# Two transformer blocks on one core: the second block's attention scores from rounded parts of queries and keys

## What is computed

```python
proj = u @ w_in[l]
qa, ka, va, qb, kb, vb, g = jnp.split(proj, SPLITS, axis=-1)
qa = rope(qa.reshape(B, Lp, SWA_Q_HEADS, HEAD_DIM), pos)
ka = rope(ka.reshape(B, Lp, SWA_KV_HEADS, HEAD_DIM), pos)
...
qb = rope(qb.reshape(B, Lp, DIFF_HEADS, 2, HEAD_DIM), pos)
kb = rope(kb.reshape(B, Lp, DIFF_HEADS, 2, HEAD_DIM), pos)
...
o_swa = windowed_gqa_sink_attention(qa, ka, va, attn_sink[l], pos, is_real)
...
o_diff = differential_attention(qb, kb, vb, lam, lambda_init, diff_subln_gain[l], is_key)
gates = jax.nn.sigmoid(g + b_gate[l])
g_swa, g_diff = gates[..., :D_MODEL], gates[..., D_MODEL:]
merged = g_swa * (o_swa @ w_branch_swa[l]) + g_diff * (o_diff @ w_branch_diff[l])
h = h + rms_norm(merged @ w_out[l], post_mix_gain[l])
```

## Time and profile before

| | |
|---|---|
| median of 3 runs | 877.63 us (877.02 to 877.80) |
| profiled execution, its own time | 877.45 us |
| its span, first to last instruction | 875.6 us |
| TensorE busy | 868.0 us, 99% |
| VectorE, ScalarE, GpSimd busy | 623.7 (71%), 459.2 (52%), 46.2 us (5%) |
| granted TensorE clock | 0.998 |
| DMA | 156.75 MB, 179 GB/s on average |

### The profile page before, as it was taken

One profiled execution on the slowest core, in us unless ns is written; L12 is line 12 of the kernel. 1 busy time (PEld: TensorE's weight loads), 2 busy tenths in 40 slices (PEclk: granted clock), 3 DMA queues, 4 the chain that ended last, 5 costly groups with the idle time before them and its releaser, 6 DMA issues.

```text
span 875.6 us, 13035 instructions
## 1 busy us (share of the span) xinstructions
PE 868.0 (99%) x4820; PEld 731.3 (84%) x4820; DVE 623.7 (71%) x987; ACT 459.2 (52%) x735; POOL 46.2 (5%) x83
## 2 busy tenths in 40 slices
PE   9999999999999999999999999999999999999997
PEld 6887788888888888889998777777888888888886
DVE  6867777765876666668855888787766876666665
ACT  6546534334644444454556777677643654444443
POOL 1000010000200000002000000132300100000000
PEclk9999999999999999999999999999999999999999
DMA  9955344553565555353683335323274365555541
GB/s 328 412 207 187 129 160 144 192 192 144 190 242 190 189 195 188 142 190 104 207 300 106 123 123 170 145 100 142 97 265 175 119 228 189 183 192 192 186 143 48
DMA packets 26830, 156.75 MB, mean 179 GB/s; under 512 B 3600, under 2 KB 5136, under 8 KB 9376
## 3 DMA queue, kind: packets, MB, share of 16 engines
q1 hardware_dynamic: 24048, 148.71, 47.6%
q10 hardware_dynamic: 2736, 7.42, 2.4%
HBM read 151.45 MB, written 1.05 MB: 174 GB/s over the span
## 4 chain that ended last, share of the span: by engine, by line
PE 99%; DMA 0%; DVE 0%; DVEq 0%; SPq 0%; ACTq 0%; ACT 0%; issue 0%
PE ps L495 19%; PE ps L497 18%; PE ps L496 18%; PE ps L661 8%; PE ps L646 8%; PE ps L665 4%; PE ps L642 4%; PE ps L674 4%; PE ps L1639 2%; PE ps L676 2%; PE ps L530 1%; PE ps L1574 1%; PE ps L1598 1%; PE ps L1593 1%; PE ps L1588 1%; PE ps L1283 1%
## 5 line engine op out<-in xcount | busy, mean ns | idle before, releaser
L1742 DVE TENSOR_TENSOR wlo<-raw,whi 128x2048 fp32r<-128x2048 f32 x134 | 306.7, 2290 | 151.7 <-ACT whi L783 151.4
L783 ACT ACTIVATE whi<-raw 128x2048 fp32r<-128x2048 f32 x134 | 256.4, 1914 | 182.8 <-PE ps L497 110.8
L495 PE MATMUL ps<-whi,xT 128*128 128x512 f32 x192 | 76.8, 400 | 0.0
L497 PE MATMUL ps<-whi,xT 128*128 128x512 f32 x192 | 75.0, 391 | 0.0
L496 PE MATMUL ps<-wlo,xT 128*128 128x512 f32 x192 | 74.8, 390 | 0.0
L495 PE MATMUL ps<-whi,fT_h 128*128 128x512 f32 x128 | 50.2, 392 | 0.0
L496 PE MATMUL ps<-wlo,fT_h 128*128 128x512 f32 x128 | 49.8, 389 | 0.0
L497 PE MATMUL ps<-whi,fT_l 128*128 128x512 f32 x128 | 49.8, 389 | 0.0
L495 PE MATMUL ps<-x_all,whi 128*128 128x272 f32 x160 | 46.6, 291 | 0.0
L496 PE MATMUL ps<-x_all,whi 128*128 128x272 f32 x160 | 46.2, 289 | 0.0
L497 PE MATMUL ps<-x_all,wlo 128*128 128x272 f32 x160 | 46.2, 289 | 0.0
(11 more groups left out here) (347 smaller groups left out, 1834.5 us busy)
## 6 DMA issues: line engine op xcount, KB each, us to landing
raw<-weights SPq DMA_DIRECT2D x134, 1024.0 KB, 4.8
kswap<-kraw SPq DMA_DIRECT2D x52, 68.0 KB, 2.0
cst<-consts SPq DMA_DIRECT2D x1, 1371.0 KB, 13.0
raw<-weights SPq DMA_DIRECT2D x4, 256.0 KB, 5.5
raw<-weights SPq DMA_DIRECT2D x2, 512.0 KB, 7.2
gate_a<-gain_rows ACTq DMA_DIRECT2D x2, 512.0 KB, 7.7
gate_r<-gain_rows ACTq DMA_DIRECT2D x2, 512.0 KB, 6.7
gate_s<-gain_rows ACTq DMA_DIRECT2D x2, 512.0 KB, 6.6
```

Source lines behind the costliest of these rows:

```text
L495: pe.matmul(o, lh, rh, start=first, stop=False)
L497: return pe.matmul(o, ll, rh, start=False, stop=last)
L783: act.activation(whi[s][:], raw[s][:], ACT.Copy).then_inc(split_hi, 1)
L1742: dve.tensor_tensor(wlo[s][:], raw[s][:], whi[s][:], ALU.subtract).then_inc(split_lo, 1)
```

## The change

**Parts instead of halves.** Queries and keys are no longer left as fp32 on 64 rows. VectorE's turning ends in `kraw` (L2343 of the changed kernel for keys, L2334 for queries, `rot_ok`). ScalarE rounds that to a high part (`keys_high`, `queries_high`, L1102, L1111, `rot_hi`), GpSimd subtracts to get the low part (L1354 for keys, L1359 for queries), and it is GpSimd that now signals `kt_ok`. The operands of the scores have 128 rows: the query tile holds the high part over the low part (or low over high for the other head of a pair), the key tile the same part twice. DMAs bring them there. Two rounded matmuls with the same weights, one with the keys' high part and one with their low part, give all four products.

**The way through memory.** A turned key of both parts is stored to a tensor in HBM (`key_parts`, `store_keys`, one DMA of 0.56 MB, five in all), and loaded from there into two key tiles of a ring (`load_shared_keys`, 2 x 6 DMAs, and `load_keys`, 8 x 4 DMAs, the latter when the scores that used the tile are done). Queries go from SBUF to SBUF (`store_queries`, 8 x 4 DMAs). All 81 are on SP's queue, between the loads and the swaps. From the third key on, `keys_high` waits until the store of the key two before it has landed, since its tile is used again.

**Order.** Query blobs are now 6, 7, 9, 10, 12, 13, 15 and 17 (the fifth of the queries in the third place), value blobs 5, 8, 11, 14 and 16. Gates and up projections alternate: 18 to 21 gates, 22 to 25 the first up projection, 26 to 29 gates, 30 to 33 the second. The units go by pairs of queries tiles (`unit_place`). The rows of the gates' bias are fetched later (steps 38 and 54), behind a wait for the scores, whose tiles they overwrite.

```diff
-QUERIES = (6, 7, 12, 13, 14, 15, 16, 17)
+QUERIES = (6, 7, 9, 10, 12, 13, 15, 17)
+QUERY_PLACE = (0, 1, 4, 2, 3, 5, 6, 7)
+VALUES = (5, 8, 11, 14, 16)
...
-VALUES_AT = {12: 0, 18: 1, 20: 2, 22: 3, 24: 4}
+VALUES_AT = {12: 0, 18: 1, 24: 2, 30: 3, 34: 4}
...
+            def store_keys(i):
+
+                sp.wait_ge(kt_ok, i + 1)
+                sp.dma_start(kd[i], knat[i % 2][:].bitcast(F32)).then_inc(kd_out[i % 2], 16)
...
+            def load_keys(cc):
+
+                sp.wait_ge(u_sc, 2 * cc + 14 if cc else 8)
+                for u in range(2):
+                    for copy in range(2):
+                        sp.dma_start(kB[cc % 2][copy * DH:(copy + 1) * DH, 2 * u:2 * u + 2, 0:KEYS],
+                                     kd[1 + cc // 2, u * DH:(u + 1) * DH, :, cc % 2, :]).then_inc(kb_in[cc % 2], 16)
...
+            def keys_high(i):
+
+                act.wait_ge(rot_ok, i + 1)
+                if i >= 2:
+
+                    act.wait_ge(kd_out[i % 2], 16 * (i // 2))
+                act.activation(knat[i % 2][:, 0], kraw[i % 2][:], ACT.Copy).then_inc(rot_hi, 1)
...
+                if q in (4, 6, 8, 10, 12):
+                    keys_high(q // 2 - 2)
...
+            for i in range(5):
+                pool.wait_ge(rot_hi, i + 1)
+                pool.tensor_tensor(knat[i % 2][:, 1], kraw[i % 2][:], knat[i % 2][:, 0],
+                                   ALU.subtract).then_inc(kt_ok, 1)
...
-                    pe.wait_ge(kt_ok, query_made(U))
+                    if t == 0:
+                        pe.wait_ge(q_in[query_of(U)], 64)
+                        pe.wait_ge(kb_in[key_slot(U)], keys_loaded(U))
...
-                    qT = qsT if U < S_UNITS else qbT
+                    qT, kT = qs if U < S_UNITS else qd, kB[key_slot(U)]
                     for u in range(2):
-                        half = slice(u * DH, (u + 1) * DH)
-                        kT = ksT[half, cc // 4, :] if U < S_UNITS else kbT[half, cc, :]
-                        m = pe.matmul(ps[:, 4 + u, 0:KEYS], qT[half, cc, t * P:(t + 1) * P], kT, start=True, stop=True)
+                        for v in range(2):
+                            m = pe.matmul(ps[:, 4 + u, 0:KEYS], qT[u][:, cc, t * P:(t + 1) * P].bitcast(F32R),
+                                          kT[:, 2 * u + v, 0:KEYS].bitcast(F32R), start=v == 0, stop=v == 1)
```

More of the change, by code:

```diff
@@ L123, in values_blob @@
 def values_blob(i):
-    return 7 + i if i else 5
+    return VALUES[i]
 def swaps_before(m2):
@@ L409, in build @@
         v_ps = sem("v_ps")
+        rot_ok = sem("rot_ok")
+        rot_hi = sem("rot_hi")
         kt_ok = sem("kt_ok")
+        kd_out = [sem("kd_out0"), sem("kd_out1")]
+        kb_in = [sem("kb_in0"), sem("kb_in1")]
+        q_in = [sem(f"q_in{j}") for j in range(len(QUERIES))]
         ql_ok = sem("ql_ok")
@@ new lines, in load_keys, with store_queries @@
+            def load_keys(cc):
+                sp.wait_ge(u_sc, 2 * cc + 14 if cc else 8)
+                for u in range(2):
+                    for copy in range(2):
+                        sp.dma_start(kB[cc % 2][copy * DH:(copy + 1) * DH, 2 * u:2 * u + 2, 0:KEYS],
+                                     kd[1 + cc // 2, u * DH:(u + 1) * DH, :, cc % 2, :]).then_inc(kb_in[cc % 2], 16)
+            def store_queries(m2):
+                i = QUERIES.index(m2)
+                sp.wait_ge(kt_ok, 5 + i + 1)
+                j = QUERY_PLACE[i]
+                both = slice(2 * (j % 4), 2 * (j % 4) + 2)
+                hi, lo, dst = qh[i % 2], ql[i % 2], qs if j < 4 else qd
+                low, high = slice(0, DH), slice(DH, P)
+                sp.dma_start(dst[0][low, both, :], hi[low].bitcast(F32)).then_inc(q_in[j], 16)
+                sp.dma_start(dst[0][high, both, :], lo[low].bitcast(F32)).then_inc(q_in[j], 16)
+                sp.dma_start(dst[1][low, both, :], lo[high].bitcast(F32)).then_inc(q_in[j], 16)
+                sp.dma_start(dst[1][high, both, :], hi[high].bitcast(F32)).then_inc(q_in[j], 16)
@@ L2481, in weight_stream @@
     out += blob_tokens(w, at[2], 256)
-    for q in range(2):
-        out += blob_tokens(qa, 256 * q, 256)
-    for q in range(4):
-        out += blob_tokens(w, at[5] + 256 * q, 256)
-    for q in range(2, 4):
-        out += blob_tokens(qa, 256 * q, 256)
-    for q in range(4):
-        out += blob_tokens(w, at[3] + 256 * q, 256)
-    for q in range(4):
-        out += blob_tokens(w, at[6] + BANK * q)
-    for up in (head_pairs(np.asarray(i["w_branch_swa_2"])[0], 0, 0), np.asarray(i["w_branch_diff_2"])[0]):
+    values = 0
+    for m2 in range(6, 18):
+        if m2 in QUERIES:
+            j = QUERY_PLACE[QUERIES.index(m2)]
+            out += blob_tokens(qa, 256 * j, 256) if j < 4 else blob_tokens(w, at[3] + 256 * (j - 4), 256)
+        else:
+            out += blob_tokens(w, at[5] + 256 * values, 256)
+            values += 1
+    for g, up in enumerate((head_pairs(np.asarray(i["w_branch_swa_2"])[0], 0, 0), np.asarray(i["w_branch_diff_2"])[0])):
+        for q in range(2):
+            out += blob_tokens(w, at[6] + BANK * (2 * g + q))
         out += blob_tokens(up, 0) + blob_tokens(up, BANK)
```

111 lines of the change are left out of this document (75 added, 36 removed).

## The result

The changed kernel takes 887.93 us (median of 4 runs, 887.28 to 889.52) beside 877.33 for the kernel before on the same chip: 1.0124 times the time, 95% interval 1.0107 to 1.0142. It is slower by 10.6 us where I had forecast 2, and lies just above the upper end of my range (887.0). The profiled execution took 889.52, with a span of 887.7; it was the slowest of the four.

A forecast was written before the change was run, and what follows sets the result against it. TensorE, busy 99% of the span, was taken to bound the kernel. From 877.45 us, -8.0 (scores) + 5.8 (roundings) + 2.2 (GpSimd parts) + 2.0 (SP's queue) = +2.0 gave 879.5 us, range 873.0 to 887.0.

The forecast's parts named there:

- (a): Scores on TensorE: four rounded 128-row matmuls per unit and fewer tile-shape changes save 8.0 us, 0.5 either way.
- (b): Key stage: ScalarE's 13 roundings and what stands behind them lose 5.8 us, between 3.0 and 8.
- keys 0 to 2: Key stage: late weight halves for blobs 4, 5 and 6 make TensorE lose 0.2, 1.2 and 0.5 us.
- keys 3 and 4: Key stage: waits for stores delay the last rounding, so TensorE gets the first values' PSUM pair 3.9 us late.
- (c): GpSimd's 13 low parts: 2.0 us each, between 0.72 and 3.8; 2.2 us in the sum for query parts.
- The 2.2 for the query parts: Units: eight GpSimd query parts between VectorE's work cost 2.2 us, from 0 to 8.
- The shared port: Rival, chance 0.17: in key stage and units, GpSimd's part stops VectorE for its length; 5.8 us more, 885.
- (d): SP's queue: 81 more DMAs, 0.6 us each to issue; 26 at blobs 12 and 13 lose 2.0 us (0 to 4).
- three signs that were to prove me wrong: Key stage loses under 2 us; VectorE never waits for GpSimd yet time rises; TensorE waits for q_in or key loads.
- mostly covered: Rival, chance 0.28: stores land early, DMA issues take 0.45; key stage costs 3.0 us, the rest 0.5, giving 873.0.
- The rounded matmuls: Scores; rival, chance 0.03: they need two passes each instead of running at 0.125, costing 16 us, 890 or more.

The follow-up runs named there:

- the version with all low parts on VectorE: The changed kernel with six edits and three more, including key stores on ScalarE's queue, a third key tile and all low parts on VectorE: 876.89 us (1.0001).

## Why the prediction was wrong

- **(a), the scores: the mechanism right, the size too large.** Slots of 4.34 against 4.70 and no 0.20 before the group in the second half came as it said. But -8.0 was forecast, with 0.5 either way, and TensorE's own work fell by 6.5 in the changed kernel. In the version with all low parts on VectorE, where no clock is lost, its busy time is 862.0 against 868.0, 6.0 less, and 5.6 us of waits leave the span where it was before. What ate the 1.5 to 2.0 us stays open; waits too short to show between TensorE's overlapping records count as busy time. This alone puts the changed kernel 1.5 us above the forecast.
- **(b), keys 0 to 2: right.** Forecast 0.2, 1.2 and 0.5; TensorE's first waits are none, 1.3 and 0.6.
- **(b), keys 3 and 4: the place was right, the size was not.** I had named the values' PSUM pair, emptied behind the last rounding, as what TensorE would wait for, and given it 3.9. It took 1.6 + 6.0. The step that failed is "a 0.56 MB store issued behind a load lands 6.3 after that load's issue", which gave landings at 435.2 and 441.1: they came at 436.5 and 445.3, 7.9 and 10.3 after the load's issue. I had worked out a landing as if a transfer met only the load just ahead of it. The stores with their loads and swaps kept the DMA engines at 0.89 from 427 to 441, where they were at 0.73 before; the store of key 2 needed 10.0 us. Leaving four stores out took 10.6 of the 13.0 us away at blob 7.
- **The clock: missing.** No term of the sum had a price for a wait beyond its length. Two waits brought 6.3 and 3.4 us at 1.2 GHz, 4.9 us of work lost; a bare pause of 3.1 in the kernel before costs 4.9 in three executions of five and about 3.1 in two.
- **(c), GpSimd: the value was about right, the bound too.** I took 2.0 for a part, between 0.72 and 3.8: it is 1.35 alone and up to 2.66 beside VectorE, and 2.11 on average for the query parts. (The estimate of 1.2 from the Trainium skill, GPSIMD Engine Reference, 3.1 Elementwise, is near the 1.35.) The 2.2 for the query parts could not be confirmed: 0.9 measured, within the noise.
- **The shared port: true, and not the main cause.** What no row had shown is now shown. VectorE's timeline in the changed kernel, beside the GpSimd parts that start at 423.40 and take 1.90, and at 429.40 and take 1.36:

```profile
423.36 0.72 DVE L2342 TENSOR_TENSOR kswap<-kswap,turn 128x544 f32<-128x544 f32 x1
424.11 1.77 DVE L2343 TENSOR_TENSOR kraw<-kraw,kswap 128x544 f32<-128x544 f32 x1
...
429.98 1.36 DVE L2341 TENSOR_TENSOR kraw<-kraw,turn 128x544 f32<-128x544 f32 x1 [1.90 <-DMA kswap<-kraw]
```

  An add and a multiply that take 0.72 else take 1.77 and 1.36: VectorE waits for GpSimd's end. (The Trainium skill, SBUF — State Buffer, Who interferes with whom, calls the shared pair of ports an exclusive lock; the trace agrees in both directions.) In the changed kernel the key parts took 1.46 on average and only these two instructions of the rotations were held up, by 1.7 us together. It is worth 3.5 us once the transfers are out of the way. That this rival's 885 lies nearer to the result than my forecast is no merit: it was not the cause, and its sum is wrong too. 3 x 1.0 + (8 x 1.0 - 2.2) is 8.8, not 5.8, which makes 888.3 and lies outside the range that was to reach beyond it.
- **(d), SP's queue: half.** The issue times were right (0.6 each, 26 in a row), and the wait came where I had put it, before unit 1. I priced it at 2.0 and it was 3.6, plus 1.7 for the clock. Again a DMA was costed by its issue and by its landing alone, where the engines were 96.6% busy.
- None of the three signs that were to prove me wrong came: the key stage lost more than 2 us, VectorE did wait for GpSimd, and nothing waited for q_in or the key loads. The sign that would have warned me, DMA share, was in no term.

The rival "mostly covered" had it that ScalarE waits under 1 us for the stores; it waited 13.3. The rounded matmuls did run 0.12 to 0.13 apart, but for the first pair of a group, 0.21.

## What to carry to other kernels

Add up what a change puts on the DMA engines in each stretch, not only what each transfer takes alone: from a share of 0.3 to one of 0.97 the landing of everything else in that stretch moves, and with it every chain that has a transfer in it. Where two chains end near the same time, removing one wait buys only what the other leaves; follow the second before pricing the first. And a long wait of TensorE can cost more than itself: 1.9 us more here by the median for one of 6.2, and for one of 3.1 about 2 or nothing, from one execution to the next.

## What was not expected of the hardware

- A TensorE wait of 3.1 us brought 1.2 GHz afterwards in the profiled execution and cost 4.9 by the median of five, in two of which the mean clock was 0.999 and nothing but the pause was lost; one of 6.2 cost 8.1.
- GpSimd's and VectorE's two-input instructions over SBUF hold each other up: 1.35 becomes 2.6 on the one, 0.72 becomes 1.4 to 1.8 on the other. The five key parts done by VectorE alone took less time on both. A GpSimd copy with one input held VectorE up as well, 0.69 to 1.10.
- ScalarE issued a store in 0.33 us. SP takes 0.6 for each of several in a row, but 0.33 to 0.47 for a load after a pause and a store behind it.
